# f32 modulation products in strips of the array, 12 of 72 in the first model's layers and 60 inside the second model's feed-forwards

## What is computed

```python
cond_x = jax.nn.silu(c)
cond_c = jax.nn.silu(c_ctx)
for layer in range(DEPTH):
    ...
    mx = jnp.split((cond_x @ mod_w[layer] + mod_b[layer])[:, None, :], N_MOD, axis=-1)
    mc = jnp.split(cond_c @ mod_w[layer] + mod_b[layer], N_MOD, axis=-1)
    x = x + 0.5 * mx[2] * swiglu(modulate(rms_norm(x, norm_g[layer, 0]), mx[0], mx[1]),
                                 ffn_w_in[layer, 0], ffn_w_out[layer, 0])
    ...
```

## Time and profile before

| | |
|---|---|
| timed runs | median 3114.78 us of 3 (3113.19 to 3118.87) |
| profiled execution, its own time (the span from its first to its last instruction) | 3115.2 us |
| PE busy | 2893.5 us, 93% |
| DVE, ACT busy | 1721.5 us (55%), 1232.1 us (40%) |
| DMA | 393 MB, 126 GB/s over the span |
| granted TensorE clock, mean | 0.954 of 2.4 GHz |
| first model | 0 to about 1275 us: two equal passes of 618 us |
| second model | from there on: feed-forward 00 (1292 to 1659), mla, 01 (1942 to 2308), 10 (2320 to 2687), swa, 11 (2899 to 3093) |

### The profile page before, as it was taken

How to read it: one execution, slowest core, us unless ns; L and a number is a source line. 1 busy time by engine, 2 the same in 40 slices (tenths; PEclk the granted TensorE clock), 3 DMA queues, 4 the chain that set the end, 5 groups by cost and what they waited for, 6 DMA issues and landing times.

```text
span 3115.2 us, 45778 instructions
## 1 busy us (share of the span) xinstructions
PE 2893.5 (93%) x17416; PEld 2520.8 (81%) x17416; DVE 1721.5 (55%) x2403; ACT 1232.1 (40%) x1488; POOL 0.2 (0%) x4
## 2 busy tenths in 40 slices
PE   7899899988998999699998898999989999889897
PEld 6888899987888999588886666888868888677897
DVE  6687667566866665624335645433353333566655
ACT  3364555443545554522323243323232232335443
POOL 0000000000000000000000000000000000000000
PEclk8999999999989999799999999999999999989998
DMA  7544467765444678224233201233232432320463
GB/s 222 157 151 153 154 210 232 220 174 149 156 143 155 211 231 232 75 70 123 74 95 87 81 1 54 75 98 111 76 86 82 115 94 79 103 68 23 135 189 101
DMA packets 584942, 393.06 MB, mean 126 GB/s; under 512 B 43670, under 2 KB 579124, under 8 KB 584628
## 3 DMA queue, kind: packets, MB, share of 16 engines
q1 hardware_dynamic: 584756, 390.57, 42.4%
HBM read 389.49 MB, written 1.05 MB: 125 GB/s over the span
## 4 chain that ended last, share of the span: by engine, by line
PE 83%; DVE 11%; ACT 4%; issue 2%; DMA 0%; SPq 0%; DVEq 0%; ACTq 0%
PE bank L1857 83%; DVE w_lo L1151 4%; ACT w_hi L837 2%; DVE t L1166 1%; DVE xs L1166 1%; DVE t L1159 1%; DVE rings L1166 1%; ACT t L841 0%; DVE acc L1159 0%; DVE h_lo L1166 0%; DMA raw<-in_w_in 0%; DVE score L1487 0%; DVE qk L1159 0%; DVE t L1163 0%; ACT gates L841 0%
## 5 line engine op out<-in xcount | busy, mean ns | idle before, releaser
L1151 DVE TENSOR_TENSOR w_lo<-raw,w_hi 128x2048 fp32r<-128x2048 f32 (+3 forms) x410 | 853.9, 2083 | 397.1 <-ACT w_hi L837 395.2
L837 ACT CAST w_hi<-raw 128x2048 fp32r<-128x2048 f32 (+3 forms) x410 | 711.8, 1737 | 691.6 <-PE bank L1857 673.2
L1857 PE MATMUL bank<-h_hi,w_hi 128*128 128x512 f32 (+1 forms) x1560 | 573.2, 367 | 51.0 <-DVE h_lo L1166 41.0
L1857 PE MATMUL bank<-h_hi,w_lo 128*128 128x512 f32 (+1 forms) x1560 | 569.1, 365 | 0.0
L1857 PE MATMUL bank<-h_lo,w_hi 128*128 128x512 f32 (+1 forms) x1560 | 568.1, 364 | 0.0
L1857 PE MATMUL bank<-x_hi,w_hi 128*128 128x256 f32 x1344 | 385.1, 287 | 20.1 <-DVE x_lo L1166 13.0
L1857 PEld LDWEIGHTS bank<-h_hi,w_hi 128*128 128x128 f32 x1560 | 297.3, 191 | 105.4 <-issue 47.8
L1857 PE MATMUL bank<-x_hi,w_lo 128*128 128x256 f32 x1344 | 378.9, 282 | 0.0
L1857 PE MATMUL bank<-x_lo,w_hi 128*128 128x256 f32 x1344 | 378.6, 282 | 0.0
L1857 PEld LDWEIGHTS bank<-h_hi,w_lo 128*128 128x128 f32 x1560 | 296.6, 190 | 49.8
L1857 PEld LDWEIGHTS bank<-h_lo,w_hi 128*128 128x128 f32 x1560 | 297.3, 191 | 47.8
(11 more groups left out here) (282 smaller groups left out, 4332.0 us busy)
## 6 DMA issues: line engine op xcount, KB each, us to landing
raw<-in_ffn_w_in SPq DMA_DIRECT2D x176, 512.0 KB
raw<-in_mod_w SPq DMA_DIRECT2D x72, 1024.0 KB
raw<-in_ffn_w_out SPq DMA_DIRECT2D x64, 704.0 KB
raw<-in_w_in SPq DMA_DIRECT2D x40, 1024.0 KB
raw<-in_w_ff_in SPq DMA_DIRECT2D x32, 1024.0 KB
raw<-in_w_ff_out SPq DMA_DIRECT2D x32, 1024.0 KB
raw<-in_w_out SPq DMA_DIRECT2D x8, 1024.0 KB
raw<-in_w_ple_gate SPq DMA_DIRECT2D x8, 1024.0 KB
```

Of the source, the lines that this page charges most:

```text
L837: act.copy(w_hi[s][:, w], raw[s][:, w]).then_inc(hi_made, c.did(hi_made))
L1151: dve.tensor_tensor(w_lo[s][:, w], raw[s][:, w], w_hi[s][:, w].bitcast(F32), ALU.subtract).then_inc(lo_made, c.did(lo_made))
L1857: ins = pe.transpose(o, l, r) if transpose else pe.matmul(o, l, r, start=start, stop=stop)
```

## The change

Nothing of what is computed changes. The modulation product is made in plain f32 from the raw chunk, so that no `w_hi` and `w_lo` of it is made:

- **Product.** `cond_st` is now f32, 32 columns for each of the eight row blocks k, two of them used. `mod_product` makes eight f32 matmuls of 256 columns, block k into the 32-partition strip k mod 4 of one bank. Each of six modulation chunks in a row stands at other partitions of the strip (`at`), DVE's `mod_row` adds it to `mod_rows` (128 x 256), and after six chunks one `mod_turn` turns and folds all of them.
- **In the layers** a pass makes six of them (12 in both), after the chunks in `MOD_AFTER`, from a buffer of its own (`mod_slot`, the idle half of `xs`).
- **In feed-forwards 00 and 01** each pass makes 12, **in 10** six, after the chunks in `FFN_MOD_AFTER`. These are loaded into the same three `raw` slots, between the main chunks (`ffn_stream`), and a slot that holds one is free for the entry three later when PE has multiplied it (`mod_full`, `slot_free`).
- **Context input.** `c_tok` is no longer loaded and turned at the start of the program, but at the end of each layer pass, inside the last layer norm.

```diff
+MOD_AFTER = [6, 10, 15, 21, 33, 37]
+MOD_TURN = 41
+SP_AHEAD = 6
...
+FFN_MOD_AFTER = [1, 2, 3, 4, 5, 6, 10, 12, 13, 14, 15, 16]
+FFN_MOD_TURN = (8, 17)
+FFN_MODS = {(0, 0): (12, 0, 12), (0, 1): (12, 1, 0), (1, 0): (6, 1, 24), (1, 1): (0, 0, 0)}
+
+def ffn_stream(unit):
+    out = []
+    for k in range(FFN_CHUNKS):
+        out.append(("main", k))
+        if k in FFN_MOD_AFTER[:FFN_MODS[unit][0]]:
+            out.append(("mod", FFN_MOD_AFTER.index(k)))
...
+            def slot_free():
+                kind, k = RING_ORDER[n[0] - SLOTS] if n[0] >= SLOTS else ("main", n[0] - SLOTS)
+                if kind == "main":
+                    sp.wait_ge(lo_made, c.value(lo_made, k + 1 + SLOTS))
+                else:
+                    sp.wait_ge(mod_full, c.value(mod_full, k + 2))
...
-                sp.wait_ge(lo_made, c.value(lo_made, n[0] + 1))
+                slot_free()
...
+            def mod_row(q):
+                dve.wait_ge(mod_full, c.next(mod_full))
+                b = d_bank()
+                if q % MOD_GROUP:
+                    dve.wait_ge(c.last, c.own())
+                    tt(mod_rows[:, :], b[:, 0:256], mod_rows[:, :], ALU.add).then_inc(d_free, c.did(d_free))
+                else:
+                    copy(mod_rows[:, :], b[:, 0:256]).then_inc(d_free, c.did(d_free))
...
+            def mod_product(q, w):
+                pe.wait_ge(rd.free, rd.awaited())
+                b = rd.claim()
+                at = 2 * (MOD_GROUP - 1 - q % MOD_GROUP)
+                span = P // COL_GROUPS
+                for k in range(KT):
+                    strip = slice(span * (k % COL_GROUPS), span * (k % COL_GROUPS + 1))
+                    mm(b[strip, 0:256], cond_st[:, at + span * k:at + span * k + span], w[:, k, :], k < COL_GROUPS, k >= KT - COL_GROUPS,
+                       mod_full if k == KT - 1 else None)
+                rows_at[0] = rd.used
+
+            def mod_turn():
+                pe.wait_ge(d_free, c.value(d_free, rows_at[0] + 1))
+                pe.sem_inc(apart, 1)
+                pe.wait_ge(rd.free, rd.awaited())
+                b = rd.claim()
+                for t in range(2):
+                    mm(b[:, 2 * MOD_GROUP * t:2 * MOD_GROUP * (t + 1)], mod_rows[:, P * t:P * t + P], fold, True, True,
+                       d_full if t else None)
...
-                    for k in range(KT):
-                        for z in range(2):
-                            mm(b[:, 0:256], cond_st[:, 4 * k:4 * k + P], w[z][:, k, :], k == 0 and z == 0, k == KT - 1 and z == 1,
-                               d_full if k == KT - 1 and z == 1 else None)
...
+                        if k in FFN_MOD_AFTER[:count]:
+                            q = FFN_MOD_AFTER.index(k)
+                            at = start + stream.index(("mod", q))
+                            pe.wait_ge(landed[at % SLOTS], c.value(landed[at % SLOTS], LANDED * (at // SLOTS + 1)))
+                            mod_product(q, raw[at % SLOTS][:, :].rearrange("p (k n) -> p k n", k=KT))
```

More of the change, by code:

```diff
@@ L100 @@
 MODS = 36
[L101 to L112, removed]
+CHUNKS1 = len(MAIN)
+assert CHUNKS1 % SLOTS == 0
+COL_GROUPS = 4
+MOD_GROUP = 6
+MODS1 = MODS // 6
+MOD_AFTER = [6, 10, 15, 21, 33, 37]
+MOD_TURN = 41
+SP_AHEAD = 6
+assert len(MOD_AFTER) == MODS1 == MOD_GROUP
 SPARSE = 11
@@ L171 @@
 assert FFN_CHUNKS % SLOTS == 0
+FFN_MOD_AFTER = [1, 2, 3, 4, 5, 6, 10, 12, 13, 14, 15, 16]
[7 more added lines that the diff above has]
+            out.append(("mod", FFN_MOD_AFTER.index(k)))
+    assert len(out) % SLOTS == 0 and all(kind == "main" for kind, _ in out[:2] + out[-3:])
+    return out
 MLA_UNITS = [(h, part) for h in range(MLA_H) for part in range(3)]
@@ L190, in chunk_widths @@
 def chunk_widths():
-    size = {"qk": 2048, "v": 2048, "gate": 2048, "up": 1536, "mod": 2048, "out": 2048, "plegate": 2048, "ple": 2048,
+    size = {"qk": 2048, "v": 2048, "gate": 2048, "up": 1536, "out": 2048, "plegate": 2048, "ple": 2048,
             "ffin": 2048, "ffout": 2048}
@@ L209, with ring_order, put @@
 WIDTHS = chunk_widths()
+def ring_order():
+    out, n = [], {"main": 0, "mod": LAYERS * MODS1}
+    def put(kinds):
+        for kind in kinds:
+            out.append((kind, n[kind]))
+            n[kind] += 1
+    put(["main"] * (LAYERS * CHUNKS1))
+    for unit, between in (((0, 0), 13), ((0, 1), 0), ((1, 0), 11), ((1, 1), 2)):
+        put([kind for kind, _ in ffn_stream(unit)] * 2 + ["main"] * between)
+    assert n["main"] == len(WIDTHS)
+    return out
+RING_ORDER = ring_order()
+RING_PLACE = {entry: at for at, entry in enumerate(RING_ORDER)}
 class Counts:
@@ L768, in unit_ffn @@
                 w_in, w_out = dram["ffn_w_in_2"][l, which], dram["ffn_w_out_2"][l, which]
+                count, layer, first = FFN_MODS[l, which]
                 for j in c.passes(f"ffn{l}{which}", 2):
-                    for t in range(HT):
+                    for kind, k in ffn_stream((l, which)):
+                        if kind == "mod":
+                            cols = bass.ds(j * (256 * count) + 256 * (first + k), 256)
+                            chunk(whole(dram["mod_w_2"][layer][:, cols], KT, 256))
+                            continue
+                        if k >= FFN_CHUNKS - KT:
+                            t = k - FFN_CHUNKS + KT
+                            chunk(whole(w_out[bass.ds(j * (HT * P), HT * P), P * t:P * t + P], HT, P))
+                            continue
+                        t = min(k, HT - 2 + (k - HT + 2) // 2)
                         g, u = (w_in[:, bass.ds(j * (HT * P) + (a + P * t), P)].rearrange("(k p) n -> p k n", p=P)
@@ L1213, in _, with inputs @@
             c.seen[a_free] = 1
-            def inputs(half):
-                for q in range(4):
+            def inputs(half, qs=range(4)):
+                for q in qs:
                     dve.wait_ge(d_full, c.next(d_full))
@@ L1281, in layer_norm @@
                 bump(s_free)
+                if meanwhile is not None:
+                    meanwhile(range(0, 2))
                 dve.wait_ge(s_full, c.next(s_full))
@@ L1631, in unit_ffn, with mod @@
                     d_at[0] = 0
+                    def mod(k):
+                        count, layer, first = FFN_MODS[l, which]
+                        for g in range(count // MOD_GROUP):
+                            if k == FFN_MOD_TURN[g]:
+                                mod_columns(layer, j, count, first + MOD_GROUP * g)
+                        if k in FFN_MOD_AFTER[:count]:
+                            mod_row(FFN_MOD_AFTER.index(k))
                     def unit_lo(t):
@@ L1938, in layer_norm_sums @@
                     mm(b[:, 0:S], ones, sq1[:, k, :], k == 0, k == KT - 1, s_full if k == KT - 1 else None)
+                if meanwhile is not None:
+                    meanwhile(range(2, 4))
             def as_made(o, w, x, made, give=None, per=1):
```

232 lines of the change are left out of this document (112 added, 120 removed).

## The result

| | before | after |
|---|---|---|
| timed median | 3113.99 us (4 runs) | 3458.47 us (4 runs, 3457.34 to 3462.41) |
| span of the profiled execution | 3115.2 us | 3460.6 us |
| mean granted clock | 0.954 | 0.908 |

The changed kernel is slower: the ratio is 1.1107, 95% interval 1.1091 to 1.1123.

The account below looks back on a forecast made before the run. PE bounds the kernel, busy 93% of the span. Feed-forward passes +565.2 us (four with 12 modulation chunks 457.6, two with six 107.6) and layers -149.6 us gave +415.6 on 3115.2: 3531 us, range 3400 to 3650.

Parts of the forecast that it names:

- The shared slots: Feed-forwards 00, 01, 10: late loads stop PE 5.4 us five times a pass; with 12 products also 8.9 thrice, 8.7 once.
- The clock: Behind each new standstill PE's clock falls between full speed and half, costing 2.6 us; 23.4 or 13 us a pass.
- The strips: PE's eight f32 products of a mod_product overlap only partly: 2.2 us together, bounds 1.1 and 3.7.
- The layers: Both layer passes: 187.2 us of modulation chunks go, 10 us taken off for waits, 27.6 us come: -149.6 us.
- the strips' rival: Four strips run at once in each mod_product, 1.1 us a product, 79 us less: 3452 us; chance 25%.
- The rival on the other side: Feed-forward products run early enough for their slots, nothing stands: 3104 us, with strips at once 3025; chance 5%.

Follow-up runs that it names:

- e1_order: The changed kernel with ACT's w_hi moved behind Silu and DVE's w_lo behind the multiply or residual in feed-forwards 00, 01 and 10: 3054.47 us, ratio 0.9799.
- e4_bank: The changed kernel with the feed-forwards' modulation products in two banks of their own (2 and 3) with their own semaphore: 3063.38 us, ratio 0.9818.
- e5_early: The changed kernel with the first six products of each feed-forward pass one tile earlier, behind tiles 0 to 5: 3213.89 us, ratio 1.0319.

## Why the prediction was right, and where its sizes were off

- **The shared slots: right.** The chain was predicted with its links and its count, nine in a pass with 12 and five in one with six. 5.4 us forecast, 5.67 measured in the first tile; among the output chunks 8.9 forecast, and PE's gap from 1293.21 (1282.33 + 10.88) to 1302.21 is 9.0. Inside this sum two errors nearly cancelled. The 0.3 us for SP was counted twice, for the 5.35 us begin at the end of `w_lo` and hold SP's issue already; but from the start of the matmul behind the product to `w_hi` it took 1129.44 - 1123.01 = 6.4 us, where the sum has 5.75, and PE's gate half took 5.85 us in place of 5.5. Three edits, each at one link (order, bank, time of the product), take standstills away: e1_order all 46, e4_bank all but four that remain at 4 us, e5_early the 30 in the tiles. That the weights themselves come in time, which the forecast implied and did not say, is what e1_order shows.
- **The clock: right, a little too dear.** 2.6 us forecast for each standstill; 2.6 by the windows behind the first and 2.4 by its matmuls' starts, but 2.3 by starts in the mean of all 46 (1.6 to 2.9). Together that is 104 us where 120 were forecast.
- **The strips: the step that failed.** It was "the two passes of one product use one strip and must follow each other, so only the second pass of one product and the first of the next can lie together", and gave 2.2 us. The trace shows 1.1 (1.2 with the slower matmul behind it), the lower bound: 72 x 1.0 = 72 us too much. The rival had it, at 25%. The Trainium skill ("TensorE: Matmul & The Clock Gate", Part 3) says that matmuls into different 32-column strips run concurrently; the trace agrees, also for two-pass f32: eight products of 0.43 us would be 3.4 us, and take 1.1. I set that rule below a picture of my own that no row showed.
- **The layers: mis-sized.** "2.60 us" for a chunk and "I take 10 us off" for waits that stay gave 177.2 us for what goes. The windows over the first layer pass, before and after (us, then PE's busy time), are:

```profile
27.30:645.90 618.60, 581.60 (x4415) 548.39 (x4415) 419.50 (x563) 292.04 (x307) 0.00 (x0) 0.96 0.60 183
24.80:549.70 524.90, 490.32 (x3801) 459.03 (x3801) 328.21 (x467) 223.62 (x272) 0.00 (x0) 0.96 0.53 157
```

  PE's busy time fell by 91.3 us in a pass and its idle time by 2.4 (37.0 to 34.6). With six products of 1.07 and a turning on the new side, 36 chunks had cost some 98 us of PE, 2.7 each, and no wait stayed in their place; the second pass says the same (PE's busy time fell by 92.3 us, its idle time by 5.1). Of the 45 us that the layers came out better, 14 are the cheaper products and turnings (27.6 forecast), 20 the chunks (197 in both passes in place of 177.2), 8 the idle time that went with them, and 4 lie ahead of the first pass and behind the second.
- **Not seen: the layout.** 3.5 us in each of six feed-forward passes, 21 us. The order of instructions does not show it; a buffer's new size does.
- **How it adds up.** On the spans the sum came out 70 us lower than forecast: -72 for the strips, -32 for the layers without their products, +21 for the layout, +8 for mla, swa and the end (mla 4 and swa 3 us longer, of which I can assign a part of mla's to the layout and nothing of swa's), +13 for the standstills (316 us where 304 had been forecast; two loads in 01 took 6.8 and 6.7 us on the chain) and -16 for the clock (104 us where 120 had been forecast). That makes -78; what is left to -70, 8 us, I can't assign. That the time met the strips' rival (3452) within 7 us is therefore partly luck.
- **The rival on the other side** ("the slots are not late", 3025 to 3104) did not come, but its number says what was to be had: e1_order gives 3054.

## What to carry to other kernels

When a transfer's slot is freed later, look not only at whether the data is in time for its consumer, but at what stands behind its preparation in each engine's program order: here the weights were in time, and only a multiply queued behind them was not. An engine that prepares far ahead should do so behind the work that others wait for now; and a new user of a two-bank ring halves the time that its neighbours have to free a bank. When a change alters the size of a buffer, time a stage that it doesn't touch, or keep the places of the buffers behind it.

## What the runs showed of the hardware

- Eight plain f32 products of 256 columns into four 32-partition strips take 1.1 us together, whether neighbours in order go to different strips or to the same.
- The place of SBUF buffers within 512 bytes changes the rate of matmuls of 512 columns by 2%: 0.2289 us from start to start in the old places and 512 bytes on, 0.2333 at 32 and at 480 bytes on, 0.2324 at 64. The weights' buffers did not move. The cost to the whole kernel was 40 us for 32 bytes and 29 us for 64.
- Behind each of the changed kernel's 46 new standstills (5.3 to 9.6 us without a matmul) the granted clock was 1.2 GHz for 3.3 to 6.2 us. By the starts of the matmuls that cost 1.6 to 2.9 us, 2.3 in the mean, and no more behind long standstills (2.1 behind those of 9 us) than behind short ones (2.3 behind those of 5 to 7 us).
